# Two heads' scores at once on row halves, a one-pass rounded mask, and stick-breaking attention by row blocks

## What is computed

```python
# banded: block n of 128 queries sees keys of blocks n-1, n, n+1
s = einsum('bnqhgd,bnkhd->bnhgqk', qb, kb) / 8
s = where(valid, s, -1e30)                      # |distance| <= 128
p = softmax(concatenate([s, sink], -1))[..., :-1]
o = einsum('bnhgqk,bnkhd->bnqhgd', p, vb)
# stick-breaking: z = q.k / 8, keys strictly before the query
log_beta = log_sigmoid(z)
log_one_minus = where(mask, log_sigmoid(-z), 0.0)
after = cumsum(log_one_minus, reverse=True) - log_one_minus
weights = where(mask, exp(log_beta + after), 0.0)
o = weights @ v
```

## Time and profile before

| what | value |
|---|---|
| median of 3 timed runs | 1744.34 us (1743.65 to 1744.95) |
| the profiled execution | 1748.23 us |
| its span | 1746.4 us |
| mean granted clock of TensorE | 0.985 |
| TensorE busy | 1677.4 us, 96% |
| VectorE busy | 834.1 us, 48% |
| ScalarE busy | 659.9 us, 38% |
| GpSimd busy | 272.5 us, 16% |

### The profile page before, as it was taken

How to read it: one execution, slowest core, us unless ns; L and a number is a source line. 1 busy time by engine, 2 the same in 40 slices (tenths; PEclk the granted TensorE clock), 3 DMA queues, 4 the chain that set the end, 5 groups by cost and what they waited for, 6 DMA issues and landing times.

```text
span 1746.4 us, 19135 instructions
## 1 busy us (share of the span) xinstructions
PE 1677.4 (96%) x7584; PEld 1316.7 (75%) x7584; DVE 834.1 (48%) x1330; ACT 659.9 (38%) x1150; POOL 272.5 (16%) x280
## 2 busy tenths in 40 slices
PE   5999999999999999999999998999999999999997
PEld 3557787777766787888888877776678788888886
DVE  5445455465356454333332224366654466666323
ACT  4332123454344433333332223455564344444221
POOL 3453305461012111000000002013210100000001
PEclk9999999999999999999999998999999999999999
DMA  6111112212121232332333322311101233233331
GB/s 225 61 61 48 49 53 86 71 49 61 60 62 48 99 107 73 97 97 97 96 97 96 97 84 65 102 60 36 37 25 61 73 97 97 97 97 97 109 97 72
DMA packets 39222, 139.51 MB, mean 80 GB/s; under 512 B 4332, under 2 KB 4972, under 8 KB 38941
## 3 DMA queue, kind: packets, MB, share of 16 engines
q1 hardware_dynamic: 39132, 138.29, 24.3%
HBM read 136.14 MB, written 2.10 MB: 79 GB/s over the span
## 4 chain that ended last, share of the span: by engine, by line
PE 87%; DVE 5%; POOL 3%; ACT 3%; issue 2%; DMA 0%; DVEq 0%; POOLq 0%; SPq 0%; ACTq 0%
PE ps L346 84%; PE ps L349 3%; ACT whi L1347 1%; POOL small L1801 1%; POOL small L1807 1%; DMA x<-in_x 0%; DVE wlo L778 0%; DVE W L1189 0%; POOL small L1804 0%; ACT junk L1359 0%; DVE st L1050 0%; DVE xs L789 0%; DVE sd L869 0%; DVE uT L922 0%; DVE uT L920 0%
## 5 line engine op out<-in xcount | busy, mean ns | idle before, releaser
L778 DVE TENSOR_TENSOR wlo<-wraw,whi 128x1024 fp32r<-128x1024 f32 (+2 forms) x220 | 267.1, 1215 | 523.9 <-ACT whi L1347 523.8
L346 PE MATMUL ps<-hThi,whi 128*128 128x512 f32 x1128 | 455.3, 404 | 2.2 <-DVE hTlo L794 1.3
L1347 ACT ACTIVATE whi<-wraw 128x1024 fp32r<-128x1024 f32 (+2 forms) x244 | 252.8, 1037 | 504.0 <-PE ps L346 498.5
L346 PE MATMUL ps<-hTlo,whi 128*128 128x512 f32 x1128 | 441.9, 392 | 0.0
L346 PE MATMUL ps<-hThi,wlo 128*128 128x512 f32 x1128 | 441.6, 392 | 0.0
L346 PEld LDWEIGHTS ps<-hThi,whi 128*128 128x128 f32 x1128 | 213.7, 189 | 58.1 <-issue 16.0
L346 PEld LDWEIGHTS ps<-hThi,wlo 128*128 128x128 f32 x1128 | 213.3, 189 | 45.7
L346 PEld LDWEIGHTS ps<-hTlo,whi 128*128 128x128 f32 x1128 | 213.7, 189 | 44.3 <-issue 2.9
L346 PE MATMUL ps<-whi,achi 128*128 128x512 f32 x352 | 136.9, 389 | 0.0
L346 PE MATMUL ps<-wlo,achi 128*128 128x512 f32 x352 | 136.9, 389 | 0.0
L346 PE MATMUL ps<-whi,aclo 128*128 128x512 f32 x352 | 136.9, 389 | 0.0
(11 more groups left out here) (270 smaller groups left out, 2199.1 us busy)
## 6 DMA issues: line engine op xcount, KB each, us to landing
wraw<-in_ws SPq DMA_DIRECT2D x236, 512.0 KB, 3.5
x<-in_x SPq DMA_DIRECT2D x4, 512.0 KB, 7.7
x<-in_x SPq DMA_DIRECT2D x1, 2048.0 KB, 8.2
out<-xs SPq DMA_DIRECT2D x8, 256.0 KB, 2.0
dec<-in_dec SPq DMA_DIRECT2D x1, 1024.0 KB, 15.2
wraw<-in_ws SPq DMA_DIRECT2D x4, 256.0 KB, 2.5
vec<-in_vec SPq DMA_DIRECT2D x1, 788.0 KB, 4.6
w<-in_w SPq DMA_DIRECT2D x1, 512.0 KB, 13.6
```

Source lines behind the costliest of these rows:

```text
L346: return t.matmul(o, l, r, start=first, stop=last)
L778: v.tensor_tensor(wlo[h][:, 0:width(i)], wraw[h][:, 0:width(i)], whi[h][:, 0:width(i)].bitcast(F32), ALU.subtract).then_inc(lo_done[h], 1)
L1347: a.activation(whi[h][:, 0:width(i)], wraw[h][:, 0:width(i)], ACT.Copy).then_inc(hi_done[h], 1)
```

## The change

- Banded attention: units go by h = 0, 4, 1, 5, 2, 6, 3, 7, and the scores of units u and u+1 are issued together in even steps; in odd steps there are none.
- Stick-breaking attention: units go by s_units, eight of n = 3, eight of n = 0, eight of n = 2, eight of n = 1; scores of two heads are issued together in even steps, into banks 4 and 5. All outputs collect in bank 7.
- The mask matmul uses identR and mkR, copies of the identity and of the table in the rounded type, made once by VectorE at the start of its stick program, behind its wait for in_F; TensorE waits for them by s_mk.
- The norms of the first three blocks move to steps 15, 23 and 31 of stick (their GpSimd parts to 13, 21, 29), the output copies on ACT to steps 12, 20, 28 and 36; the fourth stays in fox.

The new tiles and unit lists:

```diff
+    identR = sb("identR", AR + 131, [128, 128], F32R)
+    mkR = sb("mkR", AR + 131.5, [128, 128], F32R)
...
-    w_units = [(n, h) for n in range(4) for h in range(8)]
+    w_units = [(n, h) for n in range(4) for h in (0, 4, 1, 5, 2, 6, 3, 7)]
+    s_units = [(n, h) for n in (3, 0, 2, 1) for h in range(8)]
```

TensorE's window program:

```diff
-                if u < 32:
+                if u < 32 and u % 2 == 0:
                     scores(u)
+                    scores(u + 1)
```

TensorE's stick program:

```diff
-                take(4)
-                mm(ps[4][:, 0:wd], sqT[base:base + 64, j, n * 128:(n + 1) * 128], skT[base:base + 64, j, 0:wd], True, False)
-                w.wait_ge(in_mk, 16)
-                mm(ps[4][:, n * 128:wd], ident, mk[:, 512:640], False, True).then_inc(s_qk, 1)
-                free[4] = [(s_z, u + 1)]
+                for i in range(2):
+                    take(4 + i)
+                    base, j = 64 * i, s_units[u][1] // 2
+                    mm(ps[4 + i][:, 0:wd], sqT[base:base + 64, j, n * 128:(n + 1) * 128], skT[base:base + 64, j, 0:wd], True, False)
+                w.wait_ge(s_mk, 2)
+                for i in range(2):
+                    mm(ps[4 + i][:, n * 128:wd], identR[:], mkR[:], False, True).then_inc(s_qk, 1)
+                    free[4 + i] = [(s_z, u + i + 1)]
...
-                if u < 32:
+                if u < 32 and u % 2 == 0:
                     scores(u)
-                if u in (22, 25):
-                    out_norm_turn((u - 22) // 3, 6)
+                if u in (15, 23, 31):
+                    out_norm_turn((u - 15) // 8, 6)
```

VectorE's stick program:

```diff
             w.wait_ge(in_F, 32)
+            w.wait_ge(in_mk, 16)
+            v.tensor_copy(identR[:], ident).then_inc(s_mk, 1)
+            v.tensor_copy(mkR[:], mk[:, 512:640]).then_inc(s_mk, 1)
```

ScalarE's stick program:

```diff
-                a.activation(zb[u % 3][:, 0:wd], ps[4][:, 0:wd], ACT.Copy).then_inc(s_z, 1)
+                a.activation(zb[u % 3][:, 0:wd], ps[4 + u % 2][:, 0:wd], ACT.Copy).then_inc(s_z, 1)
```

More of the change, by code:

```diff
@@ L287, in build @@
         sem(n) for n in ("qk_c", "sv_c", "fv_c", "h_a", "h_v", "fl_v", "fl_a", "fl_p"))
+    s_mk = sem("s_mk")
     s_qk, s_z, s_ab, s_ln, s_sc, s_sum, s_w, s_tr, s_ev, s_pv = (
@@ L611, in scores @@
             def scores(u):
-                n, h = pairs[u]
-                base, j, wd = 64 * (h % 2), h // 2, 128 * (n + 1)
-                take(4)
-                mm(ps[4][:, 0:wd], sqT[base:base + 64, j, n * 128:(n + 1) * 128], skT[base:base + 64, j, 0:wd], True, False)
-                w.wait_ge(in_mk, 16)
-                mm(ps[4][:, n * 128:wd], ident, mk[:, 512:640], False, True).then_inc(s_qk, 1)
-                free[4] = [(s_z, u + 1)]
+                n, wd = s_units[u][0], 128 * (s_units[u][0] + 1)
+                for i in range(2):
[6 more added lines that the diff above has]
+                    free[4 + i] = [(s_z, u + i + 1)]
             def turn(u):
-                wd = 128 * (pairs[u][0] + 1)
+                wd = 128 * (s_units[u][0] + 1)
                 w.wait_ge(s_w, u + 1)
@@ L629, in values @@
             def values(u):
-                n, h = pairs[u]
-                b = 5 if n > 1 else 7
+                n, h = s_units[u]
                 w.wait_ge(s_ev, u + 1)
@@ L634, in values @@
                 if h == 0:
-                    take(b)
+                    take(7)
                 for k in range(n + 1):
-                    op = mm(ps[b][:, h * 64:(h + 1) * 64], PT2[u % 2][:, k * 128:(k + 1) * 128], sv[:, k, h * 64:(h + 1) * 64],
+                    op = mm(ps[7][:, h * 64:(h + 1) * 64], PT2[u % 2][:, k * 128:(k + 1) * 128], sv[:, k, h * 64:(h + 1) * 64],
                             k == 0, k == n)
@@ L640, in values @@
                 if h == 7:
-                    free[b] = [(o_c, (14, 15, 30, 31).index(u) + 1)]
+                    free[7] = [(o_c, u // 8 + 1)]
             for u in range(37):
@@ L696, in fox @@
                     turn(u - 3)
-                if u in (3, 7, 22, 26):
-                    out_norm_turn({3: 2, 7: 3, 22: 4, 26: 5}[u], 3)
+                if u in (7, 22, 26):
+                    out_norm_turn({7: 3, 22: 4, 26: 5}[u], 3)
                 if 5 <= u < 37:
@@ L1205, in stick @@
                     parts(u)
-                if u in (22, 25):
-                    out_norm_low((u - 22) // 3, 0, "gsb", 6)
+                if u in (15, 23, 31):
+                    out_norm_low((u - 15) // 8, 0, "gsb", 6)
                 yield
@@ L1252, in fox @@
                     evac(u - 3)
-                if u in (4, 8):
-                    out_norm_low(2 + u // 8, 0, "gsb", 3)
+                if u == 8:
+                    out_norm_low(3, 0, "gsb", 3)
                 if u in (23, 27):
@@ L1635, in copy @@
                     w.wait_ge(s_sum, u - 2)
-                a.activation(zb[u % 3][:, 0:wd], ps[4][:, 0:wd], ACT.Copy).then_inc(s_z, 1)
+                a.activation(zb[u % 3][:, 0:wd], ps[4 + u % 2][:, 0:wd], ACT.Copy).then_inc(s_z, 1)
             def logs(u):
-                L, wd = Lb[u % 5], 128 * (pairs[u][0] + 1)
+                L, wd = Lb[u % 5], 128 * (s_units[u][0] + 1)
                 w.wait_ge(s_ab, 2 * u + 1)
@@ L1656, in stick @@
                     weights(u - 2)
[L1657 to L1660, removed]
+                if u in (15, 23, 31):
+                    out_norm_high((u - 15) // 8, 0, "gsb", 6)
+                if u >= 5 and (u - 5) % 8 == 7:
+                    q = (u - 5) // 8
                     w.wait_ge(s_pv, u - 4)
@@ L1664, in stick @@
                         w.wait_ge(o_sc, 3 * q)
-                    a.activation(W5[3][:], ps[5 if q % 2 == 0 else 7][:], ACT.Copy).then_inc(o_c, 1)
+                    a.activation(W5[3][:], ps[7][:], ACT.Copy).then_inc(o_c, 1)
                     w.wait_ge(o_c, q + 1)
@@ L1693, in fox @@
                     evac(u - 3)
-                if u in (3, 7):
-                    out_norm_high(2 + u // 7, 0, "gsb", 3)
+                if u == 7:
+                    out_norm_high(3, 0, "gsb", 3)
                 if u in (22, 26):
@@ L1949, in stick @@
                 if 2 <= u < 34:
-                    wd = 128 * (pairs[u - 2][0] + 1)
+                    wd = 128 * (s_units[u - 2][0] + 1)
                     L, nr, z = Lb[(u - 2) % 5], W5[(u - 2) % 3], zb[(u - 2) % 3]
@@ L1954, in stick @@
                     g.tensor_tensor(L[:, 0:wd], z[:, 0:wd], nr[:, 0:wd], ALU.add).then_inc(s_sum, 1)
[L1955 to L1958, removed]
+                if u in (13, 21, 29):
+                    out_norm_scale((u - 13) // 8)
                 yield
```

## The result

The changed kernel takes 1729.65 us (median of four runs, 1726.5 to 1731.5) against 1744.64 for the kernel before: 15.0 us less, a ratio of 0.9907 with a 95% interval of 0.989 to 0.9923 (a range behind a ratio below is such an interval). A second set of runs (e10) gave 1731.6 against 1746.9, 0.9914 (0.9897 to 0.993). The profiled execution of the changed kernel took 1728.6, its span is 1726.8.

What follows compares the result with a forecast made beforehand. TensorE, busy for 96% of the span, bounds the kernel. Window -4.4, stick direct -18.6, stick waits 0 and front +6.9 sum to -16.1 us: 1732 from the profiled run, 1728 from the timed median; range 1715 to 1739.

Steps and rivals of the forecast that it cites:

- Pairs cost one score: Banded and stick scores: the second of a pair is free; 0.63, 0.84 or 1.05 us by width.
- Banded stage: Banded attention (window): -13.7 us gain, +8.5 new waits, +0.8 half a clock fall: -4.4; bounds 13.7 gained, 2 lost.
- The six waits: Banded attention: second scores in steps 8, 10, 16, 18 and turned blocks ahead of steps 11, 19 wait; sum 8.5 us.
- Scores and drains in the stick stage: Stick stage: paired scores save 11.7 us, score changes after turns and values 1.4, steps 1 and 3 another 0.3.
- Masks: Stick stage: one-pass rounded masks at 0.30 us a pair, 4.8 in all against about 10 before: -5.2.
- Front: Start of stick stage: TensorE idles 4.5 us for identR and mkR, low clock costs 2.4: +6.9, between 4 and 9.
- Waits in the stick stage: Stick stage: about 12 us lost to waits and low clock against 11.6 before; 0, between 6 better and 9 worse.
- The norm's turns: Stick steps 15, 23, 31: turns taking bank 6 wait bare for PT, since no score and mask lie between.
- Waits that do not come: Rival, chance 0.13: the window's 8.5 and 0.8 vanish, stick stage loses 5 less; -30, 1714 us.
- VectorE binding: Rival, chance 0.14: VectorE binds in the stick stage, loss 21 in place of 12; -7, 1737 us.
- Partial overlap: Rival, chance 0.05: a pair's second score costs a third of a single, 7.9 back; -8, 1736 us.
- Starving by small gaps: Slower rival, chance 0.07: stick stage, 25 steps wait 1 us each, six clock falls cost 1.6 each; +7, 1751 us.

Runs made afterwards that it cites:

- e10: The changed kernel, unaltered, run and profiled again against the kernel before: 1731.6 us against 1746.9.
- e4: Kernel before plus only the banded attention's change, with values of unit u-4 between a pair's two scores: 1750.3 us against 1746.2 before.
- e1: Changed kernel with VectorE making identR and mkR after the group sq, not behind its wait for in_F: 1723.9 us against 1746.2 before.
- e5: e1 with banded units 10 and 11, and 18 and 19, scored in their own steps: 1718.7 us against 1746.2 before.
- e2: Changed kernel with the float32 masks of before, waiting only for in_mk, pairs and order kept: 1726.1 us against 1746.2 before.
- e7: e1 with ScalarE's copy of full bank 7 ahead of its Exp of the weights of the same step: 1721.5 us against 1746.2 before.
- e6: e1 with the stick stage's first two output norms in steps 16 and 24 instead of 15 and 23: 1723.1 us against 1746.2 before.

## Why the prediction was right, and where it was off

The time came out 1.6 us above the forecast, and the forecast held in the main for its reasons; in the waits of the stick stage it was partly luck. By its own terms:

- **Pairs cost one score.** Held: 0.63 and 0.84 in the banded stage, 1.06 for 512 wide, as for one score. e4 shows for the banded stage that overlap is the cause. The estimate from the 3.07 of the Trainium skill, TensorE: Matmul & The Clock Gate, section Part 3, would have been 7 us poorer; for two 64-row tiles no run here shows a loss.
- **Banded stage.** -13.7 + 8.5 = -5.2 without the half fall of the clock; measured -5.3. The six waits, expected 1.1, 2.4, 1.3, 0.8, 1.7, 1.2, came at their places with 1.0, 2.4, 1.6, 0.7, 1.7, 1.3, 8.7 in all, counted as what a step takes above a pair (0.84) or two turned blocks (0.87) that wait for nothing. In this execution the clock did not fall; in e1 and e10, two of the seven profiles with these waits, it fell for 6.8 us and cost 1.6. So the 0.8, half of that, was a fair price for a matter of chance. What was not said is that 4.1 us of this could be kept at once by not pairing the two worst (e5).
- **Scores and drains in the stick stage.** -13.4, not contradicted by any row: pairs at 1.06 and 0.42 for 512 and 128. No run took these pairs apart.
- **Masks.** Taken at 0.30 a pair, measured 0.33 (0.28 and 0.05 in the values behind); -4.7 for -5.2. The rounded type alone makes 3.4 of it (e2); the rest comes with the pairing.
- **Front.** 4.5 and 2.4, together 6.9; measured 4.1 and 3.2, together 7.3 (e1). The idle time was over-, the clock's part underestimated, because only 0.4 us of the low stretch lay inside the idle time and not 1.7.
- **Waits in the stick stage, "no change, 0".** The views of waits and the cost of the time at half clock (1.6 for 3.4 us) add up to 7.2 + 3.2 = 10.4 before (PT's 6.9, and 0.3 for a copy of ScalarE's), which the prediction's count of starts has at 11.6, and without the front to 9.6 + 1.6 = 11.2 after: +0.8. The stage lengths leave +1.2 for this term: -9.6 in the stick stage and the forgetting attention together, less -13.4, -4.7 and +7.3. Both lie well inside the -6 to +9, but the 0 was in part luck. The waits that were named, for PT and the norms, are 7.0, where 12 with the clock had been forecast. The rest is a term that I did not name: all outputs now collect in bank 7, where before bank 5 took turns with it, and TensorE's first values of each block wait for ScalarE's copy: 2.6 us in three waits, and the stretch at half clock behind the second of them. I had written the norm's turns down as the only new clash of banks. e7 takes the wait for the copy away, and its stage is 3.7 shorter.
- **The norm's turns** wait 0.5, 0.7 and 0.6 for PT, as said. The reason given, that nothing stands between, is not borne out: with a score and masks between (e6) the first still waits 0.4 and the second 2.0.
- **Rivals.** Waits that do not come: no, all came. VectorE binding, with a loss of 21 us: no, the loss is 11; the stage's longest wait for PT, 1.7 us, is in step 21. Partial overlap: no. Starving by small gaps: no; TensorE waits in 13 places behind the front and not in 25 steps, and the stick stage has 10.2 us at half clock, 6.8 of them from the front.

What stays open is why VectorE's rotary sum takes 2.88 us at 359.19 and 0.68 at 362.00 for the same shape. The trace points at GpSimd: the long sum begins 0.17 after GpSimd's subtraction of 359.02 has begun and ends 0.54 after it has ended, and the two long sums of the kernel before, 2.76 at 351.01 and 2.85 at 359.93, end 0.55 behind such a subtraction too. So a good part of VectorE's lateness in step 11 is probably a wait for GpSimd, but no run here moved the one away from the other. Whether the unit order by row blocks is by itself better or worse than the old one was not tried: pairs need both heads in one block and leave one output bank.

## What to carry to other kernels

When an instruction is moved forward, ask of every bank it takes who must have emptied it, and read from the trace how late that engine is in exactly those steps; two scores side by side are free only if both banks are. A copy made once for a cheaper operand belongs where its inputs are ready, not at the head of the routine that uses it: behind an unrelated wait, two copies of 0.2 us cost 7. A pairing need not be total; leaving out the two pairs that wait was worth nearly four fifths of what the whole pairing of that stage had brought.

## What the runs showed of the hardware that was not expected

An idle time of 4.1 us came with 6.8 us of 1.2 GHz, 0.4 of them inside it, against 1.1 of 6.8 inside it in the earlier trace rows. Some stretches of this kind came and went between executions of the same kernel: the banded stage of the changed kernel had none in its first profile and 6.8 us in its second, 168.7 and 170.3 us. Others came each time: behind the two waits of step 21 of the stick stage, 1.4 to 1.7 and 1.05 us, the clock fell in six profiles of six.
